# Seven odd pairs of a mixture-of-experts stage picked on TensorE from rows in SBUF, and ten blocks of their own for the weights

## The reference, cut to what matters

```python
def _hier_moe(x, w_group, b_group, w_expert, b_expert, w1, w3, w2):
    ...  # group of the token, then its two experts and their gates -> combine (n, 32)
    acc = jnp.zeros((n, d), x.dtype)
    for e in range(N_EXPERTS):                       # 32
        hdn = jax.nn.silu(xf @ w1[e]) * (xf @ w3[e])  # w1, w3: 1024 x 512
        acc = acc + combine[:, e:e + 1] * (hdn @ w2[e])  # w2: 512 x 1024
    return acc.reshape(bsz, T, d)

x = _layer_norm(DEEPNORM_ALPHA * x + m, ln1_g, ln1_b)      # x1
f = _hier_moe(x, ...)
x = _layer_norm(DEEPNORM_ALPHA * x + f, ln2_g, ln2_b)
```

## Time and profile before

| | us |
|---|---|
| median of 3 runs | 702.8 (701.87 to 704.48) |
| the profiled execution, its own time | 704.13 |
| its span | 702.4 |
| PE busy | 598.1 (85%) |
| DVE busy | 307.2 (44%) |
| ACT busy | 217.7 (31%) |
| POOL busy | 162.4 (23%) |
| DMA queue 1 (SyncE's and ScalarE's), share of the 16 DMA engines | 77.9%, 220.92 MB |
| DMA queue 0 (GpSimd's), share of the 16 DMA engines | 5.0%, 11.78 MB |

### The profile page before, as it was taken

The page is one execution under the profiler, slowest core; times in us unless marked ns, Lnnn a source line. Parts: engine busy times, 40 slices in busy tenths (PEclk is TensorE's granted clock), DMA queues, the critical chain, the costliest instruction groups (busy, mean ns, idle before and its releaser), DMA issues.

```text
span 702.4 us, 10578 instructions
## 1 busy us (share of the span) xinstructions
PE 598.1 (85%) x4194; PEld 412.2 (59%) x4194; DVE 307.2 (44%) x785; ACT 217.7 (31%) x316; POOL 162.4 (23%) x187
## 2 busy tenths in 40 slices
PE   5999999999989899999998677777777777787782
PEld 5899999878766455555555344444434444454350
DVE  3562485616676315353535333333334433333563
ACT  3323313301212314444344231423323242414230
POOL 1000000000001223344344323222223323232242
PEclk8999999999999999999999999999999999999997
DMA  9862231835299999999999999999999999999980
GB/s 252 244 233 61 77 120 52 339 122 238 109 420 393 359 415 418 418 413 419 423 413 415 416 418 423 420 419 422 420 420 420 417 419 421 421 418 416 421 357 23
DMA packets 45786, 236.07 MB, mean 336 GB/s; under 512 B 13700, under 2 KB 18308, under 8 KB 28888
## 3 DMA queue, kind: packets, MB, share of 16 engines
q1 hardware_dynamic: 32191, 220.92, 77.9%
q0 software_dynamic: 12688, 11.78, 5.0%
q10 hardware_dynamic: 857, 2.67, 1.0%
HBM read 238.22 MB, written 30.20 MB: 382 GB/s over the span
## 4 chain that ended last, share of the span: by engine, by line
PE 46%; SPq 37%; DMA 7%; DVE 4%; issue 3%; ACT 1%; POOL 0%; POOLq 0%; DVEq 0%; ACTq 0%
SPq L400 24%; PE ps L546 14%; PE ps L721 13%; SPq L404 11%; PE ps L603 7%; PE ps L742 6%; DMA blocks<-in_w 6%; DMA blocks<-in_w_in 1%; SPq L424 1%; PE ps L632 1%; PE ps L679 1%; PE ps L707 1%; PE ps L730 1%; PE ps L616 1%; DVE blocks L1281 1%
## 5 line engine op out<-in xcount | busy, mean ns | idle before, releaser
L721 PE MATMUL ps<-blocks,ln 128*64 128x256 f32 x1952 | 228.0, 387 | 46.8 <-DMA blocks<-in_w 45.3
L721 PEld LDWEIGHTS ps<-blocks,ln 128*64 128x64 f32 x1952 | 153.6, 139 | 122.6 <-issue 71.6
L742 PE MATMUL ps<-blocks,hT 128*64 128x512 f32 x464 | 105.9, 597 | 21.5 <-DMA blocks<-in_w 20.7
L742 PEld LDWEIGHTS ps<-blocks,hT 128*64 128x64 f32 x464 | 31.8, 137 | 78.0 <-issue 49.6
L1016 ACT ACTIVATE std<-rstd,eps 128x1 f32<-128x1 f32 x32 | 9.4, 295 | 211.9 <-DVEq L1568 211.9
L1536 DVE SCALAR_TENSOR_TENSOR h_rows<-silu,slot_gate,ps 128x256 f32<-128x256 f32 x33 | 15.9, 481 | 100.8 <-PE ps L721 100.7
L1120 POOL DMA_INDIRECT prev<-first_outputs,final_row x32 | 33.9, 1058 | 75.7 <-DMA first_outputs<-ye,first_row 44.3
L1124 POOL DMA_INDIRECT out<-prev,final_row x32 | 32.1, 1002 | 82.7 <-DVE prev L1574 82.1
L966 ACT ACT_TABLE_LOAD x30 | 38.5, 1283 | 21.3 <-PE ps L721 21.0
L546 PE MATMUL ps<-xT_high,w_in_high 128*128 128x288 f32 x256 | 41.4, 305 | 4.2 <-ACT w_in_high L825 3.0
L1547 DVE TENSOR_TENSOR ye<-ye,ps 128x512 f32<-128x512 f32 x16 | 11.0, 689 | 69.4 <-PE ps L742 69.4
(11 more groups left out here) (243 smaller groups left out, 771.0 us busy)
## 6 DMA issues: line engine op xcount, KB each, us to landing
blocks<-in_w SPq DMA_DIRECT2D x85, 2048.0 KB, 42.9
tenth_block<-in_w SPq DMA_DIRECT2D x9, 2048.0 KB, 43.7
blocks<-in_w_in SPq DMA_DIRECT2D x3, 2048.0 KB, 11.6
blocks<-in_w_out SPq DMA_DIRECT2D x2, 2048.0 KB, 7.9
blocks<-in_w SPq DMA_DIRECT2D x4, 1024.0 KB, 37.6
x_tok<-in_x_prompt SPq DMA_DIRECT2D x4, 512.0 KB, 5.2
blocks<-in_w_in SPq DMA_DIRECT2D x4, 512.0 KB, 11.3
first_outputs<-in_x_prompt SPq DMA_DIRECT2D x4, 512.0 KB, 8.6
```

The lines of the kernel that those rows point to most:

```text
L721: mm = pe.matmul(ps[64 * g:64 * g + 64, bank, 0:FH], x, w[:, k, g * FH:(g + 1) * FH], start=(k == 0), stop=(k == KD - 1))
L742: mm = pe.matmul(ps[64 * g:64 * g + 64, BY, :], hT[:, k % 2, k // 2 * SLOTS:(k // 2 + 1) * SLOTS], w[:, k, g * DH:(g + 1) * DH], start=(k ...
```

## The change

- `EARLY_BLOCKS` is 10 and the tenth block has memory of its own. The memory comes from the scratch for dynamic DMAs (`dynamic_dma_scratch_size`, 16,384 bytes of each partition before, 1,024 now) and from `silu` and other small tensors being moved. Load 9 is issued right after the third slice of w_in (near 36 us in the profile before) and waits for nothing but its place in the queue.
- `x_tok` stays whole. For the pairs 3, 5, 7, 9, 11, 13 and 15 (`PICKED`) GpSimd's `fetch` is dropped. VectorE builds a 0/1 matrix `hot` of 128 slots by five groups of tokens (`make_hot`, after `final` at t = 2m - 3), TensorE multiplies it with `x_tok` in ten float32 products of 128 by 128 by 512 (`pick_pair`, after `tile(2m - 2)`), and ScalarE copies the two banks into `xe_odd` (`keep_xe`, ahead of `silu_of(2m - 1)`). `turn_pair` and `fill` of these pairs wait for `xe_kept` instead of the DMA.
- Two small VectorE operations keep each choice's tile and column (`pick_at`).
- One copy of conv rows goes through `vext[0]` instead of `equal_flat`.

```diff
-EARLY_BLOCKS = 9
+EARLY_BLOCKS = 10
+SCRATCH = 1024
+BASE = SCRATCH + 128
...
+PICKED = list(range(3, PAIRS, 2))
...
-                if n == EARLY_BLOCKS:
-                    sp.wait_ge(fetched, 1)
-                    sp.wait_ge(x1_stored, 16 * NT)
-                    return
-                kind, t = LOADS[n - EARLY_BLOCKS - 1]
+                kind, t = LOADS[n - EARLY_BLOCKS]
...
             sp.dma_start(win_a, win[:, :, 3 * DP:4 * DP]).then_inc(win_loaded[1], 16)
+            load(9)
             sp.wait_ge(w_low, 8)
...
+            def pick_pair(m):
+
+                n = PICKED.index(m)
+                pe.wait_ge(hot_ready, n + 3)
+                wait(pe, xe_kept, 2 * n)
+                pe.wait_ge(y_filled, 1)
+                for g in range(2):
+                    for j in range(NT):
+                        mm = pe.matmul(ps[:, BX[g], :], hot[:, j, :], x_tok[:, j, g * DH:(g + 1) * DH],
+                                       start=(j == 0), stop=(j == NT - 1))
+                    mm.then_inc(fetched, 1)
...
                 if t <= STAGGERED:
                     down(*place("w2", t - 1), t - 1)
+                if t % 2 == 0 and (t + 2) // 2 in PICKED:
+                    pick_pair((t + 2) // 2)
...
+            def keep_xe(m):
+                act.wait_ge(xe_turned, 2 * m - 2)
+                for g in range(2):
+                    act.wait_ge(fetched, 2 * PICKED.index(m) + g + 2)
+                    copy(xe_of[1][:, g, :], ps[:, BX[g], :]).then_inc(xe_kept, 1)
...
+                if t % 2 and (t + 1) // 2 in PICKED:
+                    keep_xe((t + 1) // 2)
                 silu_of(t)
...
-                if t % 2 == 0 and t // 2 + 2 <= PAIRS:
+                if t % 2 == 0 and t // 2 + 2 <= PAIRS and t // 2 + 2 not in PICKED:
                     fetch(t // 2 + 2)
...
+            def make_hot(m):
+
+                dve.wait_ge(fetched, 2 * PICKED.index(m) + 1)
+                for i in range(2):
+                    slot, one = pick_at[:, 2 + i, :], pick_at[:, 4, i * NT:(i + 1) * NT]
+                    settled(v.scalar_tensor_tensor(slot, pick_at[:, 0, :], float(2 * m + i), pick_at[:, 1, :],
+                                                   ALU.is_equal, ALU.mult))
+                    of = slot.rearrange("p (n k) -> p k n", k=2)
+                    settled(v.scalar_tensor_tensor(one, of[:, 0, :], -1.0, of[:, 1, :], ALU.add, ALU.add))
+                    last = v.tensor_tensor(hot[:, :, i * SLOTS:(i + 1) * SLOTS],
+                                           slots[:, :].unsqueeze(1).to_broadcast([P, NT, SLOTS]),
+                                           one.unsqueeze(2).to_broadcast([P, NT, SLOTS]), ALU.is_equal)
+                last.then_inc(hot_ready, 1)
...
                 if t > 2:
                     final(t - 2)
+                if t % 2 and (t + 3) // 2 in PICKED:
+                    make_hot((t + 3) // 2)
...
-    nc = bacc.Bacc("TRN2", target_bir_lowering=False, num_devices=1)
+    nc = bacc.Bacc("TRN2", target_bir_lowering=False, num_devices=1, dynamic_dma_scratch_size=SCRATCH)
```

More of the change, by code:

```diff
@@ L54 @@
 SECOND = (4, 6)
-BASE = 16512
+SCRATCH = 1024
+BASE = SCRATCH + 128
 X_AT = BASE
 BLOCKS_AT = X_AT + 4 * NT * D
-MIX_AT = BLOCKS_AT + 4 * 9 * BLK
+MIX_AT = BLOCKS_AT + 4 * EARLY_BLOCKS * BLK
 HOT_AT = MIX_AT + 4 * NT * D
-SMALL_AT = HOT_AT + 4 * D
+SMALL_AT = HOT_AT + 3 * D
 EARLY = 5
@@ L78 @@
 ORDERED = PLACE["w1", EARLY]
-HOME = [n % (EARLY_BLOCKS + 1) for n in range(len(LOADS))]
-LANDED = [16 * (n // (EARLY_BLOCKS + 1) + 1) for n in range(len(LOADS))]
+HOME = [n % EARLY_BLOCKS for n in range(len(LOADS))]
+LANDED = [16 * (n // EARLY_BLOCKS + 1) for n in range(len(LOADS))]
+PICKED = list(range(3, PAIRS, 2))
 def place(kind, t):
@@ L115, in build @@
         x_tok = at("x_tok", X_AT, NT, D)
-        tenth = at("tenth_block", X_AT, BLK)
-        blocks = at("blocks", BLOCKS_AT, 9, BLK)
+        blocks = at("blocks", BLOCKS_AT, EARLY_BLOCKS, BLK)
         here = BLOCKS_AT
@@ L135, in build @@
         hot_first = at("hot_first", HOT_AT, 2, NT, SLOTS)
-        silu = at("silu", HOT_AT + 4 * NT * PAIR, FH)[:, :]
-        final_row = at("final_row", HOT_AT + 4 * NT * PAIR + 4 * FH, TILES, dt=I32)
-        sample_row = at("sample_row", HOT_AT + 4 * NT * PAIR + 4 * FH + 224, TILES, dt=I32)
+        hot = at("hot", HOT_AT, NT, PAIR)
+        final_row = at("final_row", HOT_AT + 4 * NT * PAIR, TILES, dt=I32)
+        sample_row = at("sample_row", HOT_AT + 4 * NT * PAIR + 224, TILES, dt=I32)
         prev_mem = at("prev", MIX_AT, ZR, DH)
@@ L158, in build @@
         pair_row = nc.alloc_sbuf_tensor_at("pair_row", [P, PAIRS + 1], I32, offset=equal_at + 224)
+        pick_at = nc.alloc_sbuf_tensor_at("pick_at", [P, 5, 2 * NT], F32, offset=equal_at + 416)
+        silu = nc.alloc_sbuf_tensor_at("silu", [P, FH], F32, offset=equal_at + 1024)[:, :]
         second_row = nc.alloc_sbuf_tensor_at("second_row", [P, 1], I32, offset=equal_at + 384)
@@ L190, in block_at @@
         def block_at(b):
-            return tenth[:, :] if b == EARLY_BLOCKS else blocks[:, b, :]
+            return blocks[:, b, :]
         def in_block(b):
@@ L319, in build @@
         extra_ready, order_ready = sem("extra_ready"), sem("order_ready")
-        block_loaded = [sem(f"block_loaded{b}") for b in range(EARLY_BLOCKS + 1)]
+        block_loaded = [sem(f"block_loaded{b}") for b in range(EARLY_BLOCKS)]
         hot_ready = sem("hot_ready")
-        fetched = sem("fetched")
+        fetched, xe_kept = sem("fetched"), sem("xe_kept")
         xe_turned, xeT_ready = sem("xe_turned"), sem("xeT_ready")
@@ L698, in turn_second @@
                 mm.then_inc(xe_turned, 1)
+            def pick_pair(m):
[8 more added lines that the diff above has]
+                    mm.then_inc(fetched, 1)
             def turn_pair(m):
-                pe.wait_ge(x_fetched[m % 2], 16 * ((m + 1) // 2))
+                if m in PICKED:
+                    pe.wait_ge(xe_kept, 2 * PICKED.index(m) + 2)
+                else:
+                    pe.wait_ge(x_fetched[m % 2], 16 * ((m + 1) // 2))
                 pe.wait_ge(xeT_ready, 2 * m)
@@ L927, in _ @@
             copy(pooled[0:CHIST, 0:DP], ps[0:CHIST, 4, :])
-            copy(equal_flat[0:NB * CHIST, 0:DP], ps[0:NB * CHIST, 5, :]).then_inc(tail_kept, 1)
+            copy(vext[0][0:NB * CHIST, 0:DP], ps[0:NB * CHIST, 5, :]).then_inc(tail_kept, 1)
             act.wait_ge(tail_kept, 2)
             act.dma_start(conv_prompt[0], pooled[0:CHIST, 0:DP]).then_inc(tail_stored, 16)
-            act.dma_start(conv_sample.rearrange("b h c -> (b h) c"), equal_flat[0:NB * CHIST, 0:DP]).then_inc(tail_stored, 16)
+            act.dma_start(conv_sample.rearrange("b h c -> (b h) c"), vext[0][0:NB * CHIST, 0:DP]).then_inc(tail_stored, 16)
             high_of_mix(7)
@@ L1016, in spread @@
                 nc.scalar.activation(std[:, :], rstd[:, 1, 1:2], ACT.Sqrt, bias=eps[:, 1:2]).then_inc(std_ready, 1)
+            def keep_xe(m):
[3 more added lines that the diff above has]
+                    copy(xe_of[1][:, g, :], ps[:, BX[g], :]).then_inc(xe_kept, 1)
             def fill(m, i):
-                act.wait_ge(x_fetched[m % 2], 16 * ((m + 1) // 2))
+                if m in PICKED:
+                    act.wait_ge(xe_kept, 2 * PICKED.index(m) + 2)
+                else:
+                    act.wait_ge(x_fetched[m % 2], 16 * ((m + 1) // 2))
                 y_free(2 * m + i)
@@ L1497, in _ @@
             settled(v.tensor_tensor(tile_no, tile_no, near, ALU.add))
+            v.tensor_copy(pick_at[:, 0, :], tile_no)
+            v.tensor_scalar(pick_at[:, 1, :], col, 1.0, None, ALU.add)
             v.tensor_tensor(hot_col, row(slots[:, :], A), col.unsqueeze(2).to_broadcast([P, A, SLOTS]), ALU.is_equal)
```

## The result

The changed kernel takes 695.3 us (median of 15 runs, 691.3 to 699.0), the kernel before, on the same chip, 702.6 us (median of 15 runs, 699.3 to 705.1). The ratio is 0.9897 with a 95% interval from 0.9878 to 0.9915: 7.2 us less, from 6.0 to 8.6. The forecast was 697.0 with a range from 694 to 702. The profiled execution took 694.83 us, with a span of 693.1 (before: 704.13 and 702.4).

What follows compares the result with a forecast made beforehand. The weights' arrival through a full DMA queue, plus a 14.7 us tail, was taken as the bound. Fetches -5.8, load 9 0, hidden picks 0 and scratch 0 turned the median 702.8 into 697.0 us, range 694 to 702.

Steps and rivals of the forecast that it cites:

- 0 (scratch): GpSimd's DMAs with the 1 KB scratch: 2.5 under way at a time, nothing lost while three can be; 0 us.
- Fetches, -5.8: Full DMA queue after 250 us: seven dropped fetches, 2.20 MB, save between 5.3 and 6.4 us, taken as -5.8.
- Load 9, 0: SyncE's queue near 212 us: moving this load to about 36 us only leaves a hole; 0, bound -5.3 us.
- Rival C: Weight queue after 212 us: load 9 counts too, as loads behind it get in earlier; -5.3 us, 691.7; chance 0.05.
- The tail: End of the kernel, from the last half of w2 (687.7) to 702.4: 14.7 us, left alone by the change.
- The picks: TensorE between tiles: 8.6 us each, 60 us in all, hidden behind the weights; free up to 11.3 us each.
- rival D: TensorE becomes the bound from 11.3 us a pick on: 709 at 13 us, 738 at 17.2 us; chance 0.06.
- The queue at the first pick: Weight queue after tile 4: the next block release moves from 278.6 to 287.2, ten us to spare, so it stays fed.
- Rival B: DMA queue: fetches filled moments weights would not use, or it runs dry at first picks; 700 to 702.8; chance 0.12.
- First DMA-released product near tile 23: TensorE's timeline: the first product that waits for a weight load comes near tile 23 instead of tile 13.
- Small parts: VectorE, ScalarE and GpSimd side work, such as make_hot at 1.8 us each: hidden, together 0, up to +0.5 us.
- Rival E: The scratch lets only two GpSimd DMAs be under way: some 118 us slower, 815; with three, nothing; chance 0.04.

## Why the prediction was right or wrong

The total was right: 697.0 forecast, 695.3 measured, in the range and on the right side. That it came so close is in part luck. Two of its terms were wrong and a third may be, and their errors cancel: -5.8 (fetches) + 0 (load 9) + 0 (scratch) against -3.0 - 1.6 - 2.7 by the medians, and -3.3 for the scratch by the traces.

- **What bounds the kernel.** Right. With four fifths of the picks' time given back to TensorE nothing shows, a pick costs only from 11.3 us on, and seven fetches added to the queue cost their price.
- **Fetches, -5.8: too large for what arrives.** 2.20 MB left the queue, exactly as computed; put in twice, they cost 5.6 us; by the landing signals the queue is ahead by 4 to 5.5. The measured gain is 3.0, with about 1.5 to either side, and at most the 4.0 that the scratch's 3.3 leaves, should load 9 be worth nothing. The step that failed is the one from the queue's mean rate straight to the end of the program: the last signal of the last load stands between them, and, for up to 0.5 us, the last tile's chain. That these are all of the missing 1.8 to 2.8 us isn't shown.
- **Load 9, 0: the hole is there; 1.6 us by the medians, hardly clear of nothing.** Load 10 goes out at 216.65 and the hole (0.72 of the DMA's share from 200 to 217 us) is as read. Rival C, 5.3, is out. If the 1.6 us are real, their cause is open; only the last signals show them, in single traces. One guess, that w1 of tile 2 keeps its clock (3.67 us at a granted 1.00, against 5.36 in the kernel before, where it was 0.51 from 239.4 to 242.8), doesn't follow load 9: with the scratch alone it is 5.36, in the changed kernel with load 9 late 3.67, and with two products a pick and load 9 early 5.33.
- **The tail, "14.7 us that the change leaves alone": wrong.** It is 13.4 (679.71 to 693.1), and it begins at another event. The part of it behind the last landing went from 4.4 to 1.1 us with the scratch, all of it GpSimd's closing DRAIN (3.909 to 0.642 us). The term that was put at nothing is the scratch's: the prediction asked only what it has to hold, never what the kernel does with it when all work is over. Nothing excluded a gain. A span that runs 6.6 us past its last DMA's issue, when that DMA lands in 2.2, and a DRAIN of 3.9 us at its end were in the profile of the kernel before and would have been the place to look; that they hang on the scratch only a run could tell.
- **The picks.** 8.6 us forecast, 8.85 measured. Hidden, as said. The point from which they count was put at 11.3 us a pick; 13.3 us gave 709.0, where the text had 709, and 17.7 us gave 738.3, where rival D had 738 for 17.2.
- **The queue at the first pick.** No slice from the sixteenth on, in which the first pick lies, is under 414 GB/s until the last two. Rival B didn't happen in that form.
- **First DMA-released product near tile 23.** It is `down` in tile 23, at 532.96. W1 of tile 32 begins at 670.52, forecast 670.6; that it is so close is partly luck, since load 9 and the spread of executions are in it (668.2 in the second trace of the same kernel).
- **Small parts.** `make_hot` takes 1.7 us and `keep_hT` ends at 267.25, ahead of `down` at 267.39. PE busy grows by 51.8 us instead of 60: the picks are 62.0, and the other products are busy 10 us less. The kernel with neither picks nor early load 9 shows no cost of the rest.
- **Rival E.** At 1 KB not so, as forecast; at 512 bytes true. "With three, nothing" was wrong, if 512 bytes hold three: it was 16 us. An average of 2.5 in flight hides how many come at once; that these then wait for room is a reading that fits the idle time, and isn't shown.

## What to carry to other kernels

Price a transfer by its share of a full queue, but look for what is waited for at the end: the last signal of the last load, and the chain behind it, decide how much of a saving arrives. Ask of every size that a change touches what it does when the work is over, too: the time between the last landing and the end of the span is in the profile, sequencers included, and a scratch no larger than its DMAs need took 3 us off it here. Then try one size below the one chosen, as the loss began one step further down.

## What the runs showed of the hardware

- **The program's end grows with the scratch for dynamic DMAs.** GpSimd's closing DRAIN takes 3.909 us at 16 KB, 2.684 at 8 KB, 0.642 at 1 KB in all ten kernels that have it, 0.234 at 512 and at 320 bytes. From the last send to the end of the span it is 6.6, 5.4, 3.3, 2.9 and 2.9 us, with a last landing of 2.2 us at 16, 8 and 1 KB. What the DRAIN does in that time the trace doesn't show.
- **A small scratch is waited for in front of GpSimd's DMA,** as idle time that the profile calls "issue": up to 6.0 us at 512 bytes and 10.8 at 320, with instructions of 1.0 us in the median.
- **The 16 signals of one load come 5.3 to 10.8 us apart** some 490 us behind load 0 (first and last columns of the table). The Trainium skill (DMA: Bandwidth & Descriptors, "Latency and other measured facts") says that two of the 16 engines are usually slower, and offers as a guess, marked as uncertain, that GpSimd's descriptor rings load the ports that they share. No run here shows which engines lag.
- **A float32 product with a stationary of 128 columns, 512 wide,** took 0.885 us (8.85 for ten, at a granted clock of 1.00), a little above the 0.862 scaled from 288 columns.
